# Two transformer blocks on one core: the buffers of the rounded products moved to multiples of 1024 bytes in their partition

## What is computed

```python
proj = h @ w_in[l]                                        # 1024 x 7328
x = x + jnp.einsum('bsnd,bsnd->bsd', gates, up) @ w_out[l]
x = x + jnp.square(jax.nn.relu(h @ w_up[l])) @ w_down[l]  # 1024 x 4096, 4096 x 1024
...
def _swiglu(x, w_in, w_out):
    gate, up = jnp.split(x @ w_in, 2, axis=-1)            # 1024 x 5632
    return (jax.nn.silu(gate) * up) @ w_out               # 2816 x 1024
```

## Time and profile before

| | |
|---|---|
| median of 3 runs | 1994.51 us (1994.39 to 1995.58) |
| span of the profiled execution | 1993.5 us |
| TensorE matmul / weight load | 97% / 93% of the span busy |
| VectorE, ScalarE, GpSimd | 72%, 58%, 2% busy |
| TensorE on the chain that ended last | 75% |
| DMA from memory | 204 GB/s over the span |

### The profile page before, as it was taken

One profiled execution on the slowest core, in us unless ns is written; L12 is line 12 of the kernel. 1 busy time (PEld: TensorE's weight loads), 2 busy tenths in 40 slices (PEclk: granted clock), 3 DMA queues, 4 the chain that ended last, 5 costly groups with the idle time before them and its releaser, 6 DMA issues.

```text
span 1993.5 us, 37674 instructions
## 1 busy us (share of the span) xinstructions
PE 1937.0 (97%) x16000; PEld 1851.8 (93%) x16000; DVE 1442.2 (72%) x1922; ACT 1149.0 (58%) x1814; POOL 43.3 (2%) x32
## 2 busy tenths in 40 slices
PE   7999999999999999999899999899999999989999
PEld 7898899998989889999899998799999999889999
DVE  5756798888565788988756589765566657977555
ACT  6358845545436865545655565755565556566554
POOL 0100000000010000000000000000000100000000
PEclk9999999999999999999999999999999999999999
DMA  7453378996554356999455542355546554334553
GB/s 287 137 208 109 125 266 327 388 384 248 194 184 151 102 190 246 396 390 389 163 204 189 190 154 106 106 192 190 190 153 223 190 189 153 126 127 149 190 191 127
DMA packets 56182, 409.84 MB, mean 206 GB/s; under 512 B 6608, under 2 KB 6992, under 8 KB 7888
## 3 DMA queue, kind: packets, MB, share of 16 engines
q1 hardware_dynamic: 46512, 330.23, 45.8%
q10 hardware_dynamic: 9504, 77.21, 9.6%
HBM read 406.37 MB, written 1.05 MB: 204 GB/s over the span
## 4 chain that ended last, share of the span: by engine, by line
PE 75%; DVE 17%; ACT 5%; issue 2%; DMA 1%; DVEq 0%; ACTq 0%; SPq 0%
PE bank L603 24%; PE bank L605 23%; PE bank L604 23%; DVE weights_low L405 5%; DVE work L1524 2%; ACT weights_high L383 1%; DVE work L2424 1%; DVE scratch L1452 1%; ACT work L465 1%; PE bank L947 1%; DMA raw_weights<-in_stream 1%; DVE work L566 1%; DVE h_low L572 1%; ACT weights_high L384 0%; DVE work L1614 0%
## 5 line engine op out<-in xcount | busy, mean ns | idle before, releaser
L405 DVE TENSOR_TENSOR weights_low<-raw_weights,weights_high 128x1024 fp32r<-128x1024 f32 x608 | 727.8, 1236 | 353.6 <-ACT weights_high L383 347.8
L603 PE MATMUL bank<-h_high,weights_high 128*128 128x256 f32 x3024 | 854.5, 283 | 16.5 <-DVE h_low L572 11.1
L604 PE MATMUL bank<-h_low,weights_high 128*128 128x256 f32 x3024 | 841.9, 278 | 0.0
L605 PE MATMUL bank<-h_high,weights_low 128*128 128x256 f32 x3024 | 841.6, 278 | 0.0
L383 ACT ACTIVATE weights_high<-raw_weights 128x1024 fp32r<-128x1024 f32 x296 | 313.4, 1059 | 606.5 <-PE bank L605 572.5
L603 PEld LDWEIGHTS bank<-h_high,weights_high 128*128 128x128 f32 x3024 | 567.6, 188 | 34.2 <-issue 16.6
L604 PEld LDWEIGHTS bank<-h_low,weights_high 128*128 128x128 f32 x3024 | 567.4, 188 | 0.6 <-issue 0.5
L605 PEld LDWEIGHTS bank<-h_high,weights_low 128*128 128x128 f32 x3024 | 567.4, 188 | 0.0
L603 PE MATMUL bank<-weights_high,hidden_high 128*128 128x256 f32 x1280 | 359.4, 281 | 7.8 <-DVE work L2498 6.0
L605 PE MATMUL bank<-weights_high,hidden_low 128*128 128x256 f32 x1280 | 357.9, 280 | 0.0
L604 PE MATMUL bank<-weights_low,hidden_high 128*128 128x256 f32 x1280 | 357.8, 280 | 0.0
(11 more groups left out here) (304 smaller groups left out, 1864.5 us busy)
## 6 DMA issues: line engine op xcount, KB each, us to landing
raw_weights<-in_stream SPq DMA_DIRECT2D x310, 1024.0 KB, 4.8
work<-in_ada ACTq DMA_DIRECT2D x64, 1152.0 KB, 9.3
consts<-in_consts SPq DMA_DIRECT2D x1, 2048.0 KB, 12.7
work<-in_row ACTq DMA_DIRECT2D x2, 836.0 KB, 5.7
x<-in_x SPq DMA_DIRECT2D x1, 1024.0 KB, 5.0
out_x<-x SPq DMA_DIRECT2D x4, 256.0 KB, 2.2
gain_row<-in_final SPq DMA_DIRECT2D x1, 512.0 KB, 13.3
vec<-in_vec SPq DMA_DIRECT2D x1, 169.0 KB, 12.6
```

Of the source, the lines that this page charges most:

```text
L405: dve.tensor_tensor(low[:, c], raw[:, c], high[:, c].bitcast(F32), ALU.subtract).then_inc(m.raw_done[plan.index[name] % RAW], 1)
L603: pe.matmul(out, aH, bH, start=start, stop=False, skip_group_check=True)
L604: pe.matmul(out, aH, bL, start=False, stop=False, skip_group_check=True)
L605: return pe.matmul(out, aL, bH, start=False, stop=stop, skip_group_check=True)
```

## The change

`Machine.__init__` allocates the same tensors in another order, and one new tensor, `start`, of 224 float32 columns (896 bytes), which nothing uses. It fills the partition from 128 modulo 1024 to the next multiple of 1024. After it come `raw_weights`, `weights_*`, `h_*` and `hidden_*`, whose sizes are all multiples of 1024 bytes, so that each of them begins at 0 modulo 1024. `x`, `gain_row` and `mask_rounded` follow, also at 0. `mask_rounded` ends at 512 modulo 1024, so `scratch`, `work`, `consts` and `trig` begin at 512. `fox_rounded` moves behind them. No instruction, no wait and no transfer is added, removed or moved.

```diff
+        self.start = sb("start", 224)
         self.raw = sb("raw_weights", RAW * CH)
         self.wH = sb("weights_high", 2 * CH, F32R)
         self.wL = sb("weights_low", 2 * CH, F32R)
-        self.x = sb("x", 2 * D)
-        self.gain_row = sb("gain_row", D)
-        self.mask_r = sb("mask_rounded", 5 * P, F32R)
-        self.fox_r = sb("fox_rounded", 16, F32R)
         self.hH = sb("h_high", KT * T, F32R)
         self.hL = sb("h_low", KT * T, F32R)
         self.uH = sb("hidden_high", 2 * 512, F32R)
         self.uL = sb("hidden_low", 2 * 512, F32R)
+        self.x = sb("x", 2 * D)
+        self.gain_row = sb("gain_row", D)
+        self.mask_r = sb("mask_rounded", 5 * P, F32R)
         self.scratch = sb("scratch", 3072)
         self.work = sb("work", 18432)
         self.consts = sb("consts", NC)
         self.trig = sb("trig", 4 * T)
+        self.fox_r = sb("fox_rounded", 16, F32R)
```

## The result

The changed kernel takes 2039.59 us (median; 2037.63 to 2040.47), the kernel before 1994.45 us beside it: a ratio of 1.0226, 95% interval 1.0212 to 1.0241. The change makes the kernel 45 us slower. The forecast was no change, 1994 us, and the range ended at 2017.

The account below looks back on a forecast made before the run. TensorE's product spacing was taken to bound the kernel. Span 1993.5 us plus 1.0 between span and median, plus 0 for pace, spacing mix, other engines and transfers, gave 1994.5, rounded down to 1994.0 us; range 1953 to 2017.

Parts of the forecast that it names:

- What bounds the kernel: On TensorE: time is the count of products times the distance between two starts, plus some 340 us.
- Neither spacing belongs to an offset: In pe_pair and pe_down: operands at 704 and 128 swap roles, yet both kinds run at 113.3 and at 117.8 ns.
- The nearest row to the changed kernel is the before itself: TensorE products: no trace row has aligned moving operands, so neither spacing was taken to change.
- 0 for the pace: Term of the sum for TensorE's rounded products: both spacings keep their length, 0 us.
- Equal offsets collide: Rival, TensorE products: both reads hit the same place, a third spacing 4.5 ns slower; 64 us, 2058 us; chance 0.04.
- That addresses may decide the switches: At pe_down borders: swapped operand offsets, or else the banks written, might cause the spacing switch; taken as 0 us.
- a run keeping one of the two old spacings: Without switches, each TensorE run keeps its starting spacing; sum near 0; rivals short spacing 0.25, long 0.21.
- The crossing of multiples of 1024: Rival, moving reads on TensorE: without crossings products run at 108 ns; 117 us gained, 1877 us; chance 0.08.
- The other engines and transfers: ScalarE, VectorE and DMA weight transfers: taken as 0; engines worth 2 us, transfers about 20 us at most.
- The half microsecond: Rounding down of the sum, from 1994.5 to 1994.0 us, for possible gains on other engines and transfers.

Follow-up runs that it names:

- the four traces above: Kernel before (1994.5 us) and the changed kernel with h, hidden moved to 192, 64 (1988.3 us), 64, 192 (2008.0 us) and 192, 192 (1991.1 us) modulo 1024.
- e2_oldorder0: Kernel before, same tensor order, with the 896 unused bytes placed ahead: 1996.45 us, beside 1996.32 us for the kernel before.
- e3_d256: Changed kernel with 256 unused bytes added between weights_low and h_high: 2037.69 us.
- e4_d64: Changed kernel with 64 unused bytes added between weights_low and h_high: 1997.04 us, beside 1996.32 us for the kernel before.
- e10_h64_u192: Changed kernel with unused gaps that put h at 64 and hidden at 192 modulo 1024, weights at 0: 2008.0 us.

## Why the prediction was wrong

**What bounds the kernel: right.** TensorE's spacing is the time: its mean step went from 116.25 to 119.91 ns, 52.8 us over all steps, of which the span shows 42.2.

**"Neither spacing belongs to an offset": right as far as it went, and the wrong question.** I compared 128 with 704 as places, and found them alike. What matters is the distance between the two, and in the kernel before every product had the same one up to its sign, 64 or 192 modulo 256. A comparison inside one trace can't show what never varies in it. Between a product's own two operands the distance 0 did not occur once.

**The step that failed** is the last of that paragraph: "The nearest row to the changed kernel is the before itself, so I take no change of either spacing." The nearest row was no neighbour at all. The change moved all 14544 products from 64 to 0 at once. The term "0 for the pace" of the sum was 3.66 ns on each of 14426 steps, 52.8 us, and a third spacing of 120.0 ns took the place of both old ones. I named that case as a rival ("Equal offsets collide") but gave it 0.04.

**Why the rival got 0.04.** I held one step of the earlier trace rows against it: the last product of a `pe_pair` chunk, reading from 704, beside the load for the first `pe_down` product, also at 704, with a step of 113 ns. It was no odd one: 28 borders of that kind in the same trace have steps of 113 or 114 ns. But by the runs the pair that counts is rather the product and its own stationary operand, and these are 64 apart modulo 256 there too (704 against 128 or 640). If G holds, those steps never had a distance of 0, and what they excluded was less than I let them.

**The size.** I priced the collision at 4.5 ns on every product, 64 us, 2058 us. It was 119.91 - 116.25 = 3.7 ns on the mean, 52.8 us, of which 7.5 came back in shorter waits. Two terms of that price were mis-sized: the extra step (the third spacing is 2.2 ns above the long one and 6.7 above the short one, not 4.5 above each), and the shortening of waits, which I had at 0 for a loss.

**That addresses may decide the switches: a hint that held.** The prediction left open whether offsets or banks cause the switch at `pe_down`, so it can't be called right. With equal offsets the switch is gone, and the four traces above show that the offsets decide it and in which way. What I expected of that, a run keeping one of the two old spacings, did not come: at distance 0 there is neither.

**The crossing of multiples of 1024: wrong.** No steady spacing near 108 ns appeared. `e2_oldorder0` has its moving weights aligned to 1024 and runs like the kernel before. The 108 ns themselves were not measured. Line 1003 issues 8 plain float32 products there, and the trace holds 16 matmuls of 216 ns for them, so one such product takes 432 ns. Each such product shows as two matmuls where a rounded one shows as one (48 for the 48 products of a `pe_down` chunk in the window above). That each of the 216 ns holds two passes was my assumption, which no run shows; without it there is no pace of 108 ns, and nothing to say that these operands, at 704 and 128, pay nothing for their places. 113.3 ns is the fastest steady spacing in any run here.

**The other engines and transfers: right at 0.** VectorE's and ScalarE's groups after the change answer to the earlier trace rows:

```profile
L449 ACT ACTIVATE work<-work 128x512 f32<-128x512 f32 x80 | 50.6, 632 | 2.5
L466 ACT ACTIVATE work<-x 128x512 f32<-128x512 f32 x44 | 27.7, 630 | 17.2 <-DVE x L2364 8.6 <-DVE x L1704 4.0 <-DMA x<-in_x 3.8
L2364 DVE TENSOR_TENSOR x<-x,scratch 128x512 f32<-128x512 f32 x24 | 16.6, 692 | 0.8
L1615 DVE TENSOR_TENSOR work<-work,scratch 128x512 f32<-128x512 f32 x16 | 11.1, 692 | 0.5
```

632, 630, 692, 692 ns, where it was 633, 630, 692, 692. The transfers and the wait for them, against the earlier trace rows:

```profile
ACT weights_high L384 <- DMA raw_weights<-in_stream: 28.1, 9, 7.4
```

```profile
raw_weights<-in_stream SPq DMA_DIRECT2D x310, 1024.0 KB, 4.8
```

A weight chunk lands in 4.8 us as before, now at a multiple of 1024 in its partition. The wait for it fell from 33.6 to 28.1 us, in a kernel that reads memory 2% more slowly (200 against 204 GB/s over the span), so that says nothing of the transfers. The half microsecond that the sum takes off for these two parts was my estimate, and no run shows it: they showed the four means within 1 ns of before and the landing at 4.8 us.

The 0 for the pace took the two reads of a product to be independent of each other's place. The runs don't fit that: 192 bytes more or less of unused space between the two operands change the mean step of some 14200 products from 119.9 to 116.2 ns (`e3_d256`, `e4_d64`). What the runs show is the dependence on the distance; where the two reads meet, and what happens there, they don't show.

## What to carry to other kernels

Where float32r matmuls with a weight load each run back to back, treat the offset between stationary and moving operands, modulo 256 bytes, as a tuning knob. Here 64 bytes apart, to either side, was best (116.2 ns) and 0 was 3.7 ns worse (119.9); 96 bytes with h ahead was as bad as 0 (119.9). Rounding all buffers to the same large power of two is how one gets 0. Read back the address that a tensor really got: here the allocator rounded a padding of 16 bytes up to 32, and 16 was never tested because of it. And when a trace shows no effect of a quantity, look first whether that quantity ever varies in it.

## What the runs showed of the hardware that was not expected

- At equal clock, TensorE has at least three steady paces for the same rounded product of 256 columns: 113.3, 117.8 and 120.0 ns. Which one is in force depends on the two operands' distance modulo 256 bytes (120.0 at 0, the other two at 64 and 192) and, at a distance of 64 or 192, on what ran before.
- The paces 113.3 and 117.8 are sticky over hundreds of products (240 in a row at 117.8 in the windows of `e10_h64_u192`). They switch where TensorE passes between `pe_pair` and `pe_down` chunks and the moving read of the chunk entered lies 64 bytes behind the stationary one (226 of 256 such borders in the four traces), and hardly at the others (8 of 256).
- An absolute shift of all operands by 128 bytes changes nothing (2039.6 and 2039.5 us; 1994.5 and 1996.5 us with 1996.3 beside it). Distances finer than 64 bytes matter: 32 bytes give 117.3 ns on average in both runs of that layout, 96 bytes 119.4.
